# Turning the rotated queries and keys with SBUF transfers and VectorE's block transpose instead of on TensorE

## The chip, the cores and the metric

The kernel runs on one core of one Trainium2 chip. Its time is the device time of the whole program in microseconds (us), median of several runs. The engines are TensorE (PE: matmuls, and PEld: its weight loads), VectorE (DVE), ScalarE (ACT), GpSimd (POOL) and SyncE (SP), whose queue issues nearly all DMAs. SBUF and PSUM have 128 partitions; PSUM is one tensor `bank` of 8 banks of 512 floats.

## The reference

One sequence of 256 tokens with 1024 features goes through two layers of the hybrid block below, then through an attention and pooling block, a state-space and convolution block, and final norms. All is float32. The change lies in the two hybrid layers:

```
h = rmsnorm(x);  z = h @ w_in                     # 1024 x 5888
aq, ak, av, rq, rk, rv, rg, ga, gb = split(z)
aq, ak = rope_half(aq), rope_half(ak)             # 8 query heads, 2 key heads of 64
ya = sliding_window_attention(aq, ak, av) @ w_a   # window 128, 4 query heads for a key head
rq, rk = rotation of pairs(rq), same(rk)          # 4 heads of 128
r  = retention(rq, rk, rv)                        # (rq rk^T * decay) rv, in chunks of 128
yb = (norm(r) * silu(rg)) @ w_b
x  = x + (sigmoid(ga) * ya + sigmoid(gb) * yb) @ w_out
x  = x + relu(rmsnorm(x) @ w_up)^2 @ w_down
```

The scores `aq ak^T` and `rq rk^T` contract over the features of a head, so on PE both operands must stand with their features on the partitions. The product with w_in leaves them with tokens on the partitions. They have to be turned in between.

## The kernel before, in words

**Products.** Every product is computed from operands split in an upper and a lower part: three matmuls for one. The weights come in pieces of 128 x 4 x 512 floats (1 MB): SP loads piece p (line 655), ACT writes its upper part w_hi (line 1466), DVE its remainder w_lo (line 1863), and PE multiplies (lines 745 to 781). Four raw buffers form a ring: the load of piece p waits until DVE has split piece p - 4. Three split buffers form another: ACT's split of p waits until PE has used p - 3. The split halves run ahead of PE by two pieces (`step(p)` splits p + 2).

**Groups.** In a layer w_in has 12 groups of 512 columns (the fourth, AKV, 256), each of two pieces and two token tiles t of 128: RQ, RK, AQ, AKV, RV0, RV1, RG0, RG1, GA0, GA1, GB0, GB1, numbered 0 to 11. PE runs one group after the other, and after each a `window(l, g)`: the small matmuls and transposes of attention and retention. The windows of ACT and DVE run in their own order, one group later (`window(l, g - 1)` in group g). Each engine runs its instructions strictly in the order written; semaphores connect them.

**Rotation.** After groups 0 and 1 `rotate_pairs` turns rq and rk by their angles: tile 0 on DVE, with splits 7 and 8 between its steps, tile 1 on POOL. Its last two steps (lines 575 and 576) write the result back into z_ret, 1024 floats a token: 8 heads of 128. After groups 2 and 3 `rotate_halves` does the same with aq and ak (lines 590 to 600), into z_att and `ak_twice`, in which each key head stands twice.

**Turning.** In window 3 (line 975) PE transposes the 16 blocks of 128 x 128 of z_ret into four banks; in window 4 (line 986) 12 blocks of z_att and ak_twice into three. ACT copies four of the seven banks to SBUF, DVE three (lines 1547 to 1553, 1980 and 1985), as rqT, rkT, aqT and akT. In window 5 PE multiplies the retention scores (line 995), which DVE multiplies by the decay (1989), and the first attention scores (lines 1012 and 1014), on which DVE and ACT run the softmax (1937 to 1956, 1570). In group 6 and 7, RG0 and RG1, DVE evacuates PE's two output banks (line 2117), and PE's next group waits for that. Line 1032 transposes the softmax's result, line 704 belongs to the convolution at the end of the kernel: it moves 16 blocks of 32 partitions from SBUF to SBUF.

**SP.** SP's queue holds the loads in the order of their pieces, and no other DMA in this part of a layer.

Of the kernel before, what the change touches and what calls it, by code (L numbers as in the profile page):

```python
# [31 lines left out]
RET_V = 256  # L32

# [126 lines left out]
def build_program(nc, ins, consts, where, out):  # L160
    ctx = ExitStack()
    with ctx:
# [118 lines left out]
        ak_twice = area(16896, T, KV_HEADS * 2 * HEAD)  # L281
# [111 lines left out]
        ret_turned = sem("ret_turned")  # L393
        rqT_ready = sem("rqT_ready")
        rkT_ready = sem("rkT_ready")
        att_turned = sem("att_turned")
        aqT_first = sem("aqT_first")
        aqT_second = sem("aqT_second")
        akT_ready = sem("akT_ready")
# [156 lines left out]
        def rotate_pairs(eng, o, l, t, tmp, between=lambda part: None):  # L556

            for g in (RQ, RK):
                eng.wait_ge(out_free[t], l * USES + g + 1)
            heads = 2 * RET_HEADS  # L560
            z = z_ret[:, t, :]
            zp = z.rearrange("p (n d e) -> p n d e", n=heads, e=2)
            cos = tab("ret_cos")[:, t * RET_QK:(t + 1) * RET_QK].unsqueeze(1).broadcast_to([P, heads, RET_QK])
            sin = tab("ret_sin")[:, t * RET_QK:(t + 1) * RET_QK].rearrange("p (d e) -> p d e", e=2)[:, :, 0]
            sin = sin.unsqueeze(1).broadcast_to([P, heads, RET_QK // 2])
            a, b = tmp[:, 0, :], tmp[:, 1, :]
            bp = b.rearrange("p (n d e) -> p n d e", n=heads, e=2)
            o.mark(eng.tensor_tensor(a.rearrange("p (n d) -> p n d", n=heads), z.rearrange("p (n d) -> p n d", n=heads), cos, ALU.mult))
            ap = a.rearrange("p (n d e) -> p n d e", n=heads, e=2)
            between(0)  # L570
            o.mark(eng.tensor_tensor(bp[:, :, :, 0], zp[:, :, :, 1], sin, ALU.mult))
            o.mark(eng.tensor_tensor(bp[:, :, :, 1], zp[:, :, :, 0], sin, ALU.mult))
            between(1)
            o.settle()
            o.mark(eng.tensor_tensor(zp[:, :, :, 0], ap[:, :, :, 0], bp[:, :, :, 0], ALU.subtract))
            eng.tensor_tensor(zp[:, :, :, 1], ap[:, :, :, 1], bp[:, :, :, 1], ALU.add).then_inc(rot_done[t], 1)
            eng.wait_ge(rot_done[t], l + 1)

        def rotate_halves(eng, o, l, t, tmp):
# [16 lines left out]
            twice = ak_twice[:, t, :].rearrange("p (v c e d) -> p v c e d", v=KV_HEADS, c=2, e=2)  # L596
            for e, op in ((0, ALU.subtract), (1, ALU.add)):
                o.mark(eng.tensor_tensor(z[:, 0:Q_HEADS, e, :], a4[:, 0:Q_HEADS, e, :], b4[:, 0:Q_HEADS, e, :], op))
                for c in range(2):
                    last = eng.tensor_tensor(twice[:, :, c, e, :], a4[:, Q_HEADS:, e, :], b4[:, Q_HEADS:, e, :], op)  # L600
                    if e == 0 or c == 0:
                        o.mark(last)
# [7 lines left out]
        def _(sp):  # L610
# [46 lines left out]

            for l in range(DEPTH):
                for g in range(W_IN_GROUPS):
                    for half in range(2):  # L660
                        load(w_in_piece(l, g, half))
                for c in range(2):
                    load(square_piece(ins["w_a"][l], c, 0))
# [65 lines left out]
        def _(pe):  # L729
# [233 lines left out]
            def window(l, g):  # L963
# [3 lines left out]
                if g == 3:  # L967
                    if l == 0:
                        pe.wait_ge(vec_ready, 3)
                    for t in (1, 0):  # L970
                        pe.wait_ge(rot_done[t], l + 1)
                        for i in range(4):
                            for j in (2 * i, 2 * i + 1):
                                c = (j % 2) * SEQ + t * P
                                last = pe.transpose(TURN[i][:, c:c + P], z_ret[:, t, j * P:(j + 1) * P], ident)
                            if t == 0:
                                last.then_inc(ret_turned, 1)
                if g == 4:
                    for t in range(T):
                        pe.wait_ge(rope_done[t], l + 1)  # L980
                    pe.wait_ge(rqT_ready, 2 * l + 1)
                    for b, src, n in ((2, z_att, 0), (5, z_att, 2), (3, ak_twice, 0)):
                        for j in range(2):
                            for t in range(T):
                                c = j * SEQ + t * P
                                last = pe.transpose(bank[:, b, c:c + P], src[:, t, (n + j) * P:(n + j + 1) * P], ident)
                        last.then_inc(att_turned, 1)
                if g == 5:
                    pe.wait_ge(rqT_ready, 2 * l + 2)
                    pe.wait_ge(rkT_ready, 2 * l + 2)  # L990
                    pe.wait_ge(akT_ready, l + 1)
# [6 lines left out]
                    pe.wait_ge(aqT_first, l + 1)  # L998
                    pe.wait_ge(aqT_second, l + 1)
# [454 lines left out]
        def _(act):  # L1454
# [86 lines left out]
            def window(l, g):  # L1541
                if l == 0 and g == 1:
                    vectors_turned()
                if g == 3:
                    for i in range(2):
                        act.wait_ge(ret_turned, 4 * l + i + 1)
                        act.activation(rqT[:, 2 * i:2 * i + 2, :].rearrange("p h t -> p (h t)"), TURN[i], copy)\
                           .then_inc(rqT_ready, 1)
                if g == 4:
                    act.wait_ge(att_turned, 3 * l + 1)  # L1550
                    act.activation(aqT[:, 0:2, :].rearrange("p i t -> p (i t)"), bank[:, 2, :], copy).then_inc(aqT_first, 1)
                    act.wait_ge(att_turned, 3 * l + 3)
                    act.activation(akT[:, :, :].rearrange("p i t -> p (i t)"), bank[:, 3, :], copy).then_inc(akT_ready, 1)
# [299 lines left out]
        def _(dve):  # L1853
# [116 lines left out]

            def window(l, g):
# [5 lines left out]
                if g == 3:  # L1977
                    for i in range(2, 4):
                        dve.wait_ge(ret_turned, 4 * l + i + 1)
                        dve.tensor_copy(rkT[:, 2 * (i - 2):2 * (i - 2) + 2, :].rearrange("p h t -> p (h t)"), TURN[i])\  # L1980
                           .then_inc(rkT_ready, 1)
                    rotate_halves(dve, order, l, 0, z_ga)
                if g == 4:
                    dve.wait_ge(att_turned, 3 * l + 2)
                    dve.tensor_copy(aqT[:, 2:4, :].rearrange("p i t -> p (i t)"), bank[:, 5, :]).then_inc(aqT_second, 1)
                if g == 5:
                    for n in range(T):
# [102 lines left out]
            for l in range(DEPTH):  # L2090
# [12 lines left out]
                for g in range(W_IN_GROUPS):  # L2103
                    if g == 4:
                        window(l, g - 1)
                    if g != AKV and (l or g):
                        step(p + 2 * g)
                    if l == 0 and g == 1:
                        spread_dt()
                    if g != 4:  # L2110
# [548 lines left out]
```

## Time and profile before

| | |
|---|---|
| median of 3 runs | 1018.91 us (1018.56 to 1019.53) |
| span of the profiled execution, first to last instruction | 1017.5 us |
| the profiled execution's own time | the page gives its span alone; the runs' median is 1.4 us above it |
| busy: PE, DVE, ACT, POOL | 99%, 70%, 50%, 17% |
| DMA queue of SP | 180.32 MB, 52.8% of the 16 engines' span |

A busy share says how much of the span an engine had instructions in flight. PE's instructions overlap: a matmul that is listed with 0.39 us may follow the one before after 0.23 us, so what a group costs is read from its start to the start of what follows. In a timeline row the bracket at the end gives idle time before the instruction and what ended it.

### The profile page before, as it was taken

To read this page: it belongs to the slowest core of one execution; us is meant where nothing else is said; L and a number is where in the kernel's file an instruction comes from. 1 tells how busy PE (TensorE), PEld (TensorE's weight loads), DVE (VectorE), ACT (ScalarE), POOL (GpSimd) and SP (SyncE) were. 2 spreads that over 40 slices of the span, in tenths; PEclk is the share of its full clock that TensorE was granted. 3 is DMA by queue.
4 is the path that set the end of the run, shared out by engine and by line. 5 is a ranking of instruction groups with operands and counts; after the bars stand their busy time and mean duration, and the time that the engine had idled before them with its cause. 6 is when DMAs were issued, how large, how long until landed. Compare 5 with 4: busy or idle time off the path is not lost.

```text
span 1017.5 us, 13670 instructions
## 1 busy us (share of the span) xinstructions
PE 1010.2 (99%) x5709; PEld 856.6 (84%) x5709; DVE 715.8 (70%) x819; ACT 506.0 (50%) x624; POOL 170.8 (17%) x129
## 2 busy tenths in 40 slices
PE   9999999999999999999999999999999999999997
PEld 8888788888888888888788888888887899899786
DVE  5767755766566565786755767888877767789974
ACT  6545544355444445454564355444467545554352
POOL 0520010000000000430000011000000139259730
PEclk9999999999999999999999999999999999999999
DMA  9763444555556555554444457556553654345451
GB/s 339 246 218 130 166 166 143 178 175 198 183 198 195 178 169 183 186 207 166 158 134 164 166 145 259 203 196 205 190 188 135 223 192 166 124 164 146 116 187 42
DMA packets 98046, 181.29 MB, mean 178 GB/s; under 512 B 8680, under 2 KB 13888, under 8 KB 97856
## 3 DMA queue, kind: packets, MB, share of 16 engines
q1 hardware_dynamic: 97808, 180.32, 52.8%
q8 instruction: 45, 0.74, 0.3%
q14 instruction: 17, 0.14, 0.0%
q10 hardware_dynamic: 176, 0.09, 0.0%
HBM read 177.02 MB, written 1.05 MB: 175 GB/s over the span
## 4 chain that ended last, share of the span: by engine, by line
PE 96%; DMA 2%; DVE 0%; ACT 0%; SPq 0%; issue 0%; DVEq 0%; ACTq 0%
PE bank L745 14%; PE bank L747 12%; PE bank L748 12%; PE bank L1072 11%; PE bank L770 9%; PE bank L774 8%; PE bank L781 8%; PE bank L1076 6%; PE bank L1154 2%; DMA raw<-in_w_in 2%; PE bank L1378 1%; PE bank L943 1%; PE bank L752 1%; PE bank L762 1%; PE bank L1365 1%; PE bank L772 1%
## 5 line engine op out<-in xcount | busy, mean ns | idle before, releaser
L1863 DVE TENSOR_TENSOR w_lo<-arena,w_hi 128x2048 fp32r<-128x2048 f32 (+1 forms) x80 | 185.3, 2325 | 107.5 <-ACT w_hi L1466 107.1
L1863 DVE TENSOR_TENSOR w_lo<-raw,w_hi 128x2048 fp32r<-128x2048 f32 (+1 forms) x78 | 181.2, 2333 | 92.1 <-ACT w_hi L1466 92.0
L1466 ACT ACTIVATE w_hi<-raw 128x2048 fp32r<-128x2048 f32 (+1 forms) x83 | 157.0, 1892 | 105.4 <-PE bank L748 71.5
L1466 ACT ACTIVATE w_hi<-arena 128x2048 fp32r<-128x2048 f32 (+1 forms) x80 | 151.3, 1891 | 105.1 <-PE bank L748 81.3
L1072 PE MATMUL bank<-hT,w_hi 128*128 128x512 f32 x504 | 123.4, 391 | 0.0
L745 PE MATMUL bank<-w_hi,hT 128*128 128x512 f32 (+1 forms) x296 | 114.1, 386 | 0.0
L1072 PEld LDWEIGHTS bank<-hT,w_hi 128*128 128x128 f32 x504 | 92.2, 188 | 17.5
L2465 POOL TENSOR_TENSOR rstd<-mean,const 128x1 f32<-128x1 f32 (+1 forms) x16 | 9.1, 578 | 557.5 <-DVE mean L1872 388.4
L748 PE MATMUL bank<-w_hi,hT 128*128 128x512 f32 (+1 forms) x256 | 97.9, 382 | 0.0
L747 PE MATMUL bank<-w_lo,hT 128*128 128x512 f32 (+1 forms) x256 | 97.9, 382 | 0.0
L770 PE MATMUL bank<-w_hi,hT 128*128 128x512 f32 (+1 forms) x216 | 84.0, 391 | 0.5 <-ACT arena L1478 0.5
L774 PE MATMUL bank<-w_hi,hT 128*128 128x512 f32 (+1 forms) x216 | 82.1, 382 | 0.0
L745 PE MATMUL bank<-w_hi,uT_hi 128*128 128x512 f32 x192 | 74.9, 390 | 0.0
L748 PE MATMUL bank<-w_hi,uT_lo 128*128 128x512 f32 x192 | 74.7, 389 | 0.0
L747 PE MATMUL bank<-w_lo,uT_hi 128*128 128x512 f32 x192 | 74.7, 389 | 0.0
L1076 PEld LDWEIGHTS bank<-hT,w_lo 128*128 128x128 f32 x504 | 67.0, 191 | 3.9
L1076 PE MATMUL bank<-hT,w_lo 128*128 128x256 f32 x504 | 68.3, 282 | 0.0
L745 PEld LDWEIGHTS bank<-w_hi,hT 128*128 128x128 f32 x296 | 55.7, 188 | 10.9
L770 PE MATMUL bank<-w_hi,uT_hi 128*128 128x512 f32 x160 | 62.5, 391 | 0.0
L774 PE MATMUL bank<-w_hi,uT_lo 128*128 128x512 f32 x160 | 62.5, 390 | 0.0
L781 PE MATMUL bank<-w_lo,hT 128*128 128x512 f32 (+1 forms) x216 | 56.1, 382 | 0.0
L748 PEld LDWEIGHTS bank<-w_hi,hT 128*128 128x128 f32 x256 | 48.1, 188 | 9.4
(350 smaller groups left out, 1899.0 us busy)
## 6 DMA issues: line engine op xcount, KB each, us to landing
arena<-in_w_in SPq DMA_DIRECT2D x22, 1024.0 KB, 5.0
raw<-in_w_in SPq DMA_DIRECT2D x20, 1024.0 KB, 5.0
arena<-in_w_up SPq DMA_DIRECT2D x16, 1024.0 KB, 5.3
raw<-in_w_up SPq DMA_DIRECT2D x16, 1024.0 KB, 5.2
arena<-in_w_down SPq DMA_DIRECT2D x16, 1024.0 KB, 5.0
raw<-in_w_down SPq DMA_DIRECT2D x16, 1024.0 KB, 5.0
raw<-in_e_w_in SPq DMA_DIRECT2D x6, 1024.0 KB, 5.1
arena<-in_e_w_in SPq DMA_DIRECT2D x6, 1024.0 KB, 5.1
```

Source lines behind the costliest of these rows:

```text
L745: pe.matmul(dst, a_hi, b_hi, start=first, stop=False, skip_group_check=shared)
L747: pe.matmul(dst, a_hi, b_lo, start=False, stop=False, skip_group_check=shared)
L748: mm = pe.matmul(dst, a_lo, b_hi, start=False, stop=last_one, skip_group_check=shared)
L752: pe.matmul(dst, a_hi, b_lo, start=False, stop=False, skip_group_check=shared)
L770: pe.matmul(dst, a_hi, b_hi, start=(start and i == 0), stop=False, skip_group_check=shared)
L774: pe.matmul(dst, a_lo, b_hi, start=False, stop=False, skip_group_check=shared)
L781: mm = pe.matmul(dst, a_hi, b_lo, start=False, stop=last_one, skip_group_check=shared)
L1072: pe.matmul(UP[j], w_hi[:, s[i], kk, at[j]], hT[:, k, :, :].rearrange("p e t -> p (e t)"), start=(i == kk == 0), stop=False, skip_group_ch ...
L1076: return pe.matmul(UP[j][:, 0:SEQ], w_lo[:, s[i], kk, at[j]], hT_hi[:, i * KP + kk, :], start=False, stop=(i == 1 and kk == KP - 1), skip_ ...
L1154: last = pe.matmul(OUT[t], a[:, KP * i + k, at[t]], w[:, s[i], k, :], start=(first and k == 0), stop=(last_one and k == KP - 1))
L1466: act.activation(w_hi[:, p % SPLIT_RING, :, 0:n], raw_at(p)[:, :, 0:n], copy).then_inc(hi_ready, 1)
L1863: dve.tensor_tensor(w_lo[:, s, :, 0:n], raw_at(p)[:, :, 0:n], w_hi[:, s, :, 0:n].bitcast(F32), ALU.subtract).then_inc(lo_ready, 1)
```

## The change

PE's 28 transposes of a layer and the seven bank copies are gone. For each of the two operands a chain of three steps takes their place. First, the last step of each rotation writes the features in another order: z_ret is then four runs of 256 floats, one for each block b of 32 features, holding that block of all eight heads; the halves go to a new area `a_rows` with four runs of 192 floats (four pairs of query heads and the two key heads, doubled). Second, SP moves run b of the token rows 32i to 32i + 31 to the partitions 32b to 32b + 31 of slot i: sixteen transfers for i and b from 0 to 3, both token tiles in each, 64 KB a transfer for the retention operand, 48 KB for the attention operand. They stand in SP's order after the loads of pieces 12 and 13 (retention, i = 0, 1 and 2, 3) and of 14 and 15 (attention), and wait for both rotations of their operand. Third, one DVE block transpose (32 x 32 blocks) per operand writes `rT` and `aT`, which lie where rqT and rkT, and aqT and akT lay. DVE waits for the sixteen retention transfers at the head of group 5, ahead of split 12, and for the attention transfers behind split 12, ahead of split 13. PE's window 5 waits for rT_ready ahead of the retention scores, and for aT_ready ahead of the attention scores.

```diff
 rotate_pairs, last two steps (rotate_halves likewise, into a_rows)
-            o.mark(eng.tensor_tensor(zp[:, :, :, 0], ap[:, :, :, 0], bp[:, :, :, 0], ALU.subtract))
-            eng.tensor_tensor(zp[:, :, :, 1], ap[:, :, :, 1], bp[:, :, :, 1], ALU.add).then_inc(rot_done[t], 1)
+            to = z.rearrange("p (b n d e) -> p n b d e", b=BLOCKS, n=heads, e=2)
+            a5, b5 = (v.rearrange("p n (b d) e -> p n b d e", b=BLOCKS) for v in (ap, bp))
+            o.mark(eng.tensor_tensor(to[:, :, :, :, 0], a5[:, :, :, :, 0], b5[:, :, :, :, 0], ALU.subtract))
+            eng.tensor_tensor(to[:, :, :, :, 1], a5[:, :, :, :, 1], b5[:, :, :, :, 1], ALU.add).then_inc(rot_done[t], 1)
...
 SP
+            def move_rows(i, dst, src, width, done):
+                rows_i = slice(i * BLOCK, (i + 1) * BLOCK)
+                for b in range(BLOCKS):
+                    rows_b = slice(b * BLOCK, (b + 1) * BLOCK)
+                    sp.dma_start(dst[rows_b], src[rows_i, :, b * width:(b + 1) * width]).then_inc(done, 16)
+            def blocks_moved(l, piece):
+                if piece in (12, 13):
+                    for t in range(T):
+                        sp.wait_ge(rot_done[t], l + 1)
+                    for i in (2 * piece - 24, 2 * piece - 23):
+                        move_rows(i, r_moved.rearrange("p (t i) x -> p t i x", t=T)[:, :, i, :], z_ret, 2 * RET_HEADS * BLOCK, r_blocks)
+                if piece in (14, 15):
+                    for t in range(T):
+                        sp.wait_ge(rope_done[t], l + 1)
+                    for i in (2 * piece - 28, 2 * piece - 27):
+                        move_rows(i, a_moved.rearrange("p (t i) x -> p t i x", t=T)[:, :, i, :], a_rows, A_SLOTS * BLOCK, a_blocks)
...
                         load(w_in_piece(l, g, half))
+                        blocks_moved(l, 2 * g + half)
...
 PE, window
-                if g == 3: 16 transposes of z_ret
-                if g == 4: 12 transposes of z_att and ak_twice
                 if g == 5:
+                    pe.wait_ge(rT_ready, l + 1)
...
+                    pe.wait_ge(aT_ready, l + 1)
...
 DVE
+            def turn_blocks(dst, src, slots):
+                return dve.transpose(dst.rearrange("p s (u q) -> p u s q", q=BLOCK), src.rearrange("p u (s f) -> p u s f", s=slots))
...
+                    if g == 5:
+                        dve.wait_ge(r_blocks, 16 * BLOCKS * BLOCKS * (l + 1))
+                        turn_blocks(rT, r_moved, 2 * RET_HEADS).then_inc(rT_ready, 1)
                     if g != AKV and (l or g):
                         step(p + 2 * g)
...
+                    if g == 5:
+                        dve.wait_ge(a_blocks, 16 * BLOCKS * BLOCKS * (l + 1))
+                        turn_blocks(aT, a_moved, A_SLOTS).then_inc(aT_ready, 1)
```

## Rows read from the trace of the kernel before

**Rows 1.** The page: busy times, granted clock in 40 slices, chain that ended last.

```profile
PE 1010.2 (99%) x5709; PEld 856.6 (84%) x5709; DVE 715.8 (70%) x819; ACT 506.0 (50%) x624; POOL 170.8 (17%) x129
...
PEclk9999999999999999999999999999999999999999
...
PE 96%; DMA 2%; DVE 0%; ACT 0%; SPq 0%; issue 0%; DVEq 0%; ACTq 0%
```

**Rows 2.** Waits of PE in all (engine, line, waited for: us, times, longest).

```profile
PE bank L850 <- DVE h_sb L1897: 1.0, 1, 1.0
```

**Rows 3.** Timeline of PE at its transposes (start, us, engine, line, operation).

```profile
48.32 1.91 PE L975 MATMUL bank<-const,arena 128*128 128x128 f32 x16
...
49.99 0.48 PE L770 MATMUL bank<-w_hi,hT 128*128 128x512 f32 x1
...
61.01 1.47 PE L986 MATMUL bank<-const,arena 128*128 128x128 f32 x12
...
446.78 1.47 PE L986 MATMUL bank<-const,arena 128*128 128x128 f32 x12
...
448.01 0.48 PE L770 MATMUL bank<-w_hi,hT 128*128 128x512 f32 x1
```

**Rows 4.** Timeline of DVE in layer 1.

```profile
433.88 0.69 DVE L576 TENSOR_TENSOR arena<-arena 128x512 f32<-128x512 f32 x1
...
436.81 1.28 DVE L1980 COPY arena<-bank 128x512 f32<-128x512 f32 x2
...
438.01 1.00 DVE L590 TENSOR_TENSOR arena<-arena,const 128x640 f32<-128x640 f32 x1
...
444.07 4.49 DVE L1863 TENSOR_TENSOR w_lo<-raw,w_hi 128x2048 fp32r<-128x2048 f32 x2
...
449.51 2.29 DVE L1863 TENSOR_TENSOR w_lo<-arena,w_hi 128x2048 fp32r<-128x2048 f32 x1 [0.94 <-ACT w_hi L1466]
...
451.72 0.68 DVE L1985 COPY arena<-bank 128x512 f32<-128x512 f32 x1
...
463.95 1.28 DVE L1989 TENSOR_TENSOR arena<-bank,const 128x512 f32<-128x512 f32 x2
...
473.79 1.28 DVE L2117 SCALAR_TENSOR_TENSOR arena<-arena,bank 128x512 f32<-128x512 f32 x2
```

**Rows 5.** Timeline of SP's queue: DMA issues.

```profile
436.92 0.37 SPq L655 DMA_DIRECT2D arena<-in_w_in  x1
...
607.41 0.98 SPq L677 DMA_DIRECT2D arena<-in_o_c_re  x1
...
928.88 5.28 SPq L704 DMA_DIRECT2D arena<-arena  x8
```

**Rows 6.** Line 704, the SBUF to SBUF transfers (issue ns min/median/max; landing).

```profile
L704 SPq DMA_DIRECT2D arena<-arena x16: 591/607/1078, 928.9 to 940.1; - x16
...
DMA to landing us min/median/max: 2.8/5.0/8.8
```

**Rows 7.** Two-microsecond stretches: busy of each engine, clock, DMA share, GB/s.

```profile
942.00:944.00 2.00, 2.00 (x20) 1.87 (x22) 1.91 (x2) 0.57 (x1) 0.76 (x1) 1.00 1.08 195
```

**Rows 8.** The page's DMA issues (count, size, us from issue to landing).

```profile
raw<-in_w_in SPq DMA_DIRECT2D x20, 1024.0 KB, 5.0
```

**Rows 9.** Timeline of ACT in layer 1, splits of pieces 13 and 14.

```profile
453.84 1.92 ACT L1466 ACTIVATE w_hi<-arena 128x2048 fp32r<-128x2048 f32 x1 [3.39 <-PE bank L748]
...
459.81 1.90 ACT L1466 ACTIVATE w_hi<-raw 128x2048 fp32r<-128x2048 f32 x1
```

**Rows 10.** Timeline of POOL, the last step of its rotation.

```profile
443.18 0.78 POOL L600 TENSOR_TENSOR arena<-arena 128x64 f32<-128x64 f32 x2
```

**Rows 11.** Timeline of PE from group 5 to group 7.

```profile
459.02 1.95 PE L995 MATMUL bank<-arena 128*128 128x128 f32 x16
...
460.90 0.49 PE L1012 MATMUL bank<-arena 64*128 64x128 f32 x4
...
475.28 0.48 PE L770 MATMUL bank<-w_hi,hT 128*128 128x512 f32 x1
```

More of the change, by code:

```diff
@@ L32 @@
 RET_V = 256
+BLOCK = 32
+BLOCKS = P // BLOCK
+A_SLOTS = PAIRS + KV_HEADS
 ATT2_HEADS = 4
@@ L280, in build_program @@
         s_ret = area(15872, T, RET_HEADS * P)
-        ak_twice = area(16896, T, KV_HEADS * 2 * HEAD)
+        rT = area(13312, 2 * RET_HEADS, SEQ)
+        aT = area(11776, PAIRS + KV_HEADS, SEQ)
+        r_moved = area(5632, T * BLOCKS, 2 * RET_HEADS * BLOCK)
+        a_moved = area(15360, T * BLOCKS, A_SLOTS * BLOCK)
+        a_rows = area(16896, T, BLOCKS * A_SLOTS * BLOCK)
         probs = area(18432, 2, 384)
@@ L392, in build_program @@
         rope_done = [sem(f"rope_done{t}") for t in range(T)]
[L393 to L399, printed above, removed]
+        r_blocks = sem("r_blocks")
+        rT_ready = sem("rT_ready")
+        a_blocks = sem("a_blocks")
+        aT_ready = sem("aT_ready")
         tanh_ready = sem("tanh_ready")
@@ L595, in rotate_halves @@
             o.settle()
-            twice = ak_twice[:, t, :].rearrange("p (v c e d) -> p v c e d", v=KV_HEADS, c=2, e=2)
+            to = a_rows[:, t, :].rearrange("p (c e s d) -> p s c e d", c=2, e=2, s=A_SLOTS)
+            aq, bq = (v[:, 0:Q_HEADS, :, :].rearrange("p (i c) e d -> p i c e d", c=2) for v in (a4, b4))
             for e, op in ((0, ALU.subtract), (1, ALU.add)):
-                o.mark(eng.tensor_tensor(z[:, 0:Q_HEADS, e, :], a4[:, 0:Q_HEADS, e, :], b4[:, 0:Q_HEADS, e, :], op))
+                o.mark(eng.tensor_tensor(to[:, 0:PAIRS, :, e, :], aq[:, :, :, e, :], bq[:, :, :, e, :], op))
                 for c in range(2):
-                    last = eng.tensor_tensor(twice[:, :, c, e, :], a4[:, Q_HEADS:, e, :], b4[:, Q_HEADS:, e, :], op)
+                    last = eng.tensor_tensor(to[:, PAIRS:, c, e, :], a4[:, Q_HEADS:, e, :], b4[:, Q_HEADS:, e, :], op)
                     if e == 0 or c == 0:
@@ L966, in window @@
                     turn_vectors()
-                if g == 3:
+                if g == 5:
+                    pe.wait_ge(rT_ready, l + 1)
                     if l == 0:
                         pe.wait_ge(vec_ready, 3)
[L970 to L991, printed above, removed]
                     for n in range(T):
@@ L997, in window @@
                         last.then_inc(s_ret_done, 1)
-                    pe.wait_ge(aqT_first, l + 1)
-                    pe.wait_ge(aqT_second, l + 1)
+                    pe.wait_ge(aT_ready, l + 1)
                 if g == 6:
@@ L1543, in window @@
                     vectors_turned()
[L1544 to L1553, printed above, removed]
                 if 6 <= g < 6 + PAIRS:
@@ L1977, in window @@
                 if g == 3:
[L1978 to L1981, printed above, removed]
                     rotate_halves(dve, order, l, 0, z_ga)
-                if g == 4:
-                    dve.wait_ge(att_turned, 3 * l + 2)
-                    dve.tensor_copy(aqT[:, 2:4, :].rearrange("p i t -> p (i t)"), bank[:, 5, :]).then_inc(aqT_second, 1)
                 if g == 5:
+                    dve.wait_ge(aT_ready, l + 1)
                     for n in range(T):
@@ L2109, in _ @@
                         spread_dt()
+                    if g == 5:
+                        dve.wait_ge(a_blocks, 16 * BLOCKS * BLOCKS * (l + 1))
+                        turn_blocks(aT, a_moved, A_SLOTS).then_inc(aT_ready, 1)
                     if g != 4:
```

## The prediction, made before the changed kernel ran

> **What bounds the kernel now.** I read the page first: the busy shares, the chain that ended last and the granted clock [rows 1]. TensorE (PE) is busy for 99% of the span, the chain that ended last is 96% PE, and the clock is at its upper level (2.4 GHz) in all 40 slices. The waits of PE come next: the longest is 1.0 us at the very start [rows 2]. So in both layers PE is the engine that sets the end, each microsecond of PE work taken out is a microsecond gained, and each wait that PE is given is a microsecond lost. The timelines of PE, VectorE (DVE), ScalarE (ACT), GpSimd (POOL) and SyncE's queue (SP) around the change give the rest. I work in the times of layer 1, whose rows are shown; layer 0 has the same pattern 385.8 us earlier (446.78 - 61.01) [rows 3]. Pieces are numbered inside the layer: group g of w_in uses pieces 2g and 2g+1.
>
> **What goes.** On PE, 16 transposes after group 3 (1.67 us from the first to the next matmul, 49.99 - 48.32) and 12 after group 4 (1.23 us, 448.01 - 446.78) [rows 3]; 2.90 us a layer, 5.8 us in all, every bit of it on the path. On DVE go the two copies after group 3 (1.20 us from their start to that of the next instruction) and one of 0.68 us after group 4 [rows 4]. ACT loses four copies; ACT waits for PE around there, so they are worth nothing. The cosine and sine products stay and the last two steps of each rotation write the same number of elements to other places; I count nothing, since the rotations are followed by slack on the paths below unless they grew by over 0.5 us.
>
> **What comes.** SP issues 32 SBUF to SBUF transfers a layer: sixteen for the retention operand (64 packets of 1 KB each, 64 KB), sixteen for the attention operand (64 packets of 768 B, 48 KB), in batches of eight behind the loads of pieces 12, 13, 14 and 15. DVE gets two block transposes, of 2048 and of 1536 elements per partition. PE gets two waits, DVE two, SP two kinds. What is queued behind them: on SP the loads of pieces 13 to 16, on DVE the weight splits 12 and 13, then the scores' softmax and the evacuations of group 6, on PE everything.
>
> *Price of an issue.* The nearest row is the sixteen SBUF to SBUF transfers late in this kernel, also 32 partitions each with three dimensions on both sides: 0.607 us of SP each, and 0.66 from one to the next (eight in 5.28 us) [rows 5, 6]. The loads cost 0.37 [rows 5] (0.41 with the gap), the dearest comparable small transfer 0.98 [rows 5]. I take 0.66, since it shares source, destination and partition count; 0.41 and 0.98 are the ends.
>
> *Price of the data.* The first of those transfers (142 KB) landed 2.8 us after issue [rows 6], and with the DMA engines full they moved 195 GB/s [rows 7]. That is 0.33 us for 64 KB and 0.25 for 48 KB: less than the 0.66 that SP takes to issue one, so SP's issuing sets the pace. A load lands 5.0 us after issue [rows 8].
>
> A rule that speaks against this change is in the Trainium skill (SBUF — State Buffer, "Door 1: The DMA port swizzle"): a transfer whose partitions are 0 to 31 reaches only 8 of 16 ports, with an asymptote of about 218 GB/s; the trace agrees, with 195. By the page's figure the sixteen 64 KB transfers would be 4.8 us (an estimate) and by the row 5.4; both lie below the issue time.
>
> *Price of a block transpose.* No row shows one. DVE's split of 2048 elements takes 2.21 us from start to start, two of them 4.49 [rows 4]. At that rate the two turns cost 2.2 and 1.7 us. The lower end is half of that (1.1 and 0.85), the upper end twice the split's, 4.4 and 3.4, for an instruction that reorders and of which no row is seen. I take 2.2 and 1.7. The Trainium skill (Vector Engine (DVE) Microarchitecture Reference, "The reshape front-end and per-opcode configuration") says that the transposing array sustains one element per cycle and lane; that agrees with the rate I took, and no run here shows it yet.
>
> **The sum, step by step in layer 1.**
> 1. Rotation of token tile 0 ends at 433.88 + 0.69 = 434.6 on DVE [rows 4]. SP issues retention batch one from 434.6 to 439.9 (8 x 0.66), load 13 to 440.3 (before it was issued at 436.9 [rows 5]; its split by ACT starts at 453.8 [rows 9], 2.9 us earlier now, and it lands by 446, so this costs nothing), batch two to 445.6.
> 2. DVE: without the two copies the rotation of halves and split 10 run 1.2 us earlier, split 10 ends at 445.1, split 11 at 447.3. PE starts group 5 at 446.78 - 1.67 = 445.1 and needs split 10 some 1.9 us later: no stall. POOL's half of the rotation ends at 443.18 + 0.78 = 444.0 [rows 10], before SP gets to it.
> 3. The last retention transfer is issued at 444.9 and lands at about 447.5. DVE arrives at 447.3, turns until 449.7, splits piece 12 until 451.9: as before (449.51 + 2.29 = 451.8 [rows 4]). This wait is free.
> 4. SP: load 14 until 446.0, attention batch one until 451.3, load 15 until 451.7, batch two until 457.0. Its eighth is issued at 456.3. It lands 2.8 us later, less 0.4 for the smaller size: 458.7. (By the data: load 15 lands at 456.3, eight transfers of 0.25 behind it end at 458.3. The same.)
> 5. DVE has stood at that wait since 451.9. It turns until 460.5.
> 6. PE: group 5 takes 11.0 us (448.01 to 459.02), so it ends at 456.1; the retention products, 1.88 us [rows 11], are done at 458.0. Then PE waits for the turned attention operand until 460.6: **a stall of 2.6 us**, and the scores start 0.3 us before their old 460.90 [rows 11]. Nearly the whole gain is given back here.
> 7. DVE comes late to what follows. Splits 13 and 14 run from 460.5 to 464.9. Piece 14 is not ACT's fault: its upper part was done at 461.7 and now is earlier [rows 9]. The decay multiply starts at 464.95 instead of 463.95 [rows 4], 1.0 us late, and the softmax and evacuation chain up to the first evacuation of group 6 runs without slack worth naming (473.79 + 0.6 = 474.4 before [rows 4]). It ends at 475.4, PE wants the bank at 475.28 - 0.3 = 475.0 [rows 11]: **a second stall of about 0.5 us**. Group 7 starts at 475.5, 0.2 us later than before. From there each chain had 2 us or so of slack or follows PE.
>
> Per layer +0.2 us, twice +0.4 us. The profiled execution's span was 1017.5 us, 1.4 below the median of the runs (1018.91); that part lies around the span and does not change. 1018.9 + 0.4 = **1019.3 us**.
>
> **The rivals.**
> *A, the issues are cheap* (0.41 each, like a load). Then SP is idle before load 14, which waits for split 10 at 445.1; attention batch two is issued by 452.6, and the data set the pace: load 14 off the engines at about 449, 2.0 us of transfers, load 15 2.6, 2.0 more and 1.0 to report: 456.6. Turned at 458.4; PE stalls 0.4, DVE is 1.05 us early at the decay multiply, PE then waits 0.6 at group 7. Net -1.85 a layer, 1015.2 us. For it: 64 packets per transfer instead of 128. Against it: a load has 512 packets and costs 0.37, so the count of packets is not what costs. No stall at all would be -5.8, 1013.1 us: the bound.
>
> *B, slower: the wait for the attention blocks grows.* The place is step 6, the price is one for one beyond 2.9 us of stall, and it decides from an issue interval of 0.66 on: 31 issues stand one behind the other between 434.6 and the last, so each further 0.1 us costs PE about 3 us a layer. At 0.8 the last attention transfer is issued at 460.6 and lands at 463.0, the scores start 3.9 us late, group 7 adds 0.4: +8.6 us in all, 1027.5. At 0.98 it is issued at 466.2, and the time is 1038.7. For it: within the second batch of the late transfers issues stretched up to 1.08 us [rows 6] while a load was ahead of them in the queue, as one is here. Against it: the first batch kept to 0.66, and these transfers are a third to a half of the size.
>
> *C, slower: a block transpose at half rate.* Turn two ends at 462.1 and the decay multiply starts 2.6 us late; scores +1.3, group 7 +0.5: +3.6 us in all, 1022.5. Nothing in the trace speaks for or against it.
>
> That PE's transposes would still be there is no rival: the code that issues them is gone. A clock that falls in a stall of several microseconds would make B worse; the trace of before has no stall that could show it [rows 1, 2].
>
> **How the numbers follow.** From no change a measurement of this kernel can tell about 0.2%, 2.0 us. My forecast 0.42, all of it within 2 us; A 0.25, faster; B 0.20 and C 0.13, slower. Range for 8 in 10: 1014.6 (below A's value, above its bound) to 1026.0 (C, and B up to an interval of about 0.77).
>
> **What would show it.** Right: L975 and L986 gone, PE waiting two to three microseconds before its first score matmul of each layer, with the DVE transpose as releaser, DVE idle for some 6 us ahead of the 1536-element transpose with a DMA as releaser, SP issuing without a break from the end of the rotation for 22 us, a short PE wait for the DVE evacuation at group 7. Wrong: no PE wait at the scores (then A), a wait of over 4 us or one before the retention products (then B), a transpose of over 3 us (then C). The forecast is also wrong if a load of pieces 13 to 17 arrives too late for ACT, which I count at nothing because the nearest, 13 and 14, have about 5 us to spare.

## The result: 1026.95 us, slower than before

The changed kernel takes 1026.95 us (four runs, 1024.84 to 1028.65) against 1018.82 (four runs of the kernel before beside them): ratio 1.0079, 95% interval [1.0064, 1.0093]. The forecast was 1019.3, the range ended at 1026.0. The profiled execution took 1025.95 us, of which the span is 1024.0, 6.5 us more than the span of before; the four runs' median is 1.0 us above it.

The page of the changed kernel, for [rows 1]: PE's share falls from 99 to 98%, one slice of the clock shows less than full, and DVE, DMA and SP are now on the chain that ended last.

```profile
PE 1008.5 (98%) x5653; PEld 853.1 (83%) x5653; DVE 721.9 (70%) x817; ACT 502.2 (49%) x616; POOL 170.7 (17%) x129
...
PEclk9999999999999999998999999999999999999999
...
PE 90%; DVE 4%; DMA 3%; SPq 2%; issue 1%; ACT 1%; DVEq 0%; ACTq 0%
```

PE's waits, for [rows 2]: the first line is new, one wait a layer, 4.4 and 3.8 us, for the turned attention operand.

```profile
PE bank L1018 <- DVE arena L1969: 8.3, 2, 4.4
PE bank L878 <- DVE h_sb L1893: 1.0, 1, 1.0
```

The chain of work in layer 0, from split 10 on (start, length, what; some of the issues left out). I tell layer 0 from here; 385.8 us lie between its times and those of layer 1 in the kernel before. After split 10 comes the load of piece 14, then issue after issue on SP's queue, the flight of the last block, the turn, and the scores.

```profile
58.02 2.30 DVE w_lo L1859
60.34 0.37 SPq L662
...
60.81 0.59 SPq L670
...
65.94 0.59 SPq L662
...
66.62 0.59 SPq L670
...
71.11 3.21 DMA arena<-arena
74.35 1.79 DVE arena L1969
```

DVE's timeline, for [rows 4]: the two block transposes take 2.31 and 1.78 us; before the second DVE stands still for 7.4 us. The first product of the rotation of halves takes 2.20 us instead of 1.00 [rows 4].

```profile
50.75 2.20 DVE L596 TENSOR_TENSOR arena<-arena,const 128x640 f32<-128x640 f32 x1
...
62.43 2.31 DVE L1969 STREAM_TRANSPOSE arena<-arena 128x2048 f32<-128x2048 f32 x1
...
74.35 1.78 DVE L1969 STREAM_TRANSPOSE arena<-arena 128x1536 f32<-128x1536 f32 x1 [7.43 <-DMA arena<-arena]
```

PE's timeline, for [rows 11]: retention products, wait, scores, group 6. In the windows under it the granted clock is the third number from the right: it falls to its lower level (1.2 GHz) while PE stands still and stays there for 6.8 us (the share of each window that is missing from 1.00, counted double). While it is low, the eight products from 77.76 to the L809 group take 3.52 us; the same eight of group 6's second token tile take 1.81 at the upper level.

```profile
69.82 1.95 PE L1002 MATMUL bank<-arena 128*128 128x128 f32 x16
76.18 0.80 PE L1018 MATMUL bank<-arena 64*128 64x128 f32 x4 [4.41 <-DVE arena L1969]
...
77.76 0.79 PE L798 MATMUL bank<-w_hi,hT 128*128 128x512 f32 x1
...
81.28 1.08 PE L809 MATMUL bank<-w_lo,hT 128*128 128x512 f32 x4
```

```profile
72.00:76.00 4.00, 0.00 (x0) 0.00 (x0) 1.65 (x1) 0.51 (x1) 0.00 (x0) 0.80 0.52 151
76.00:80.00 4.00, 3.82 (x13) 2.75 (x14) 4.00 (x3) 0.00 (x0) 0.00 (x0) 0.50 0.49 148
80.00:84.00 4.00, 4.00 (x16) 3.24 (x15) 3.83 (x8) 0.00 (x0) 0.00 (x0) 0.85 1.00 375
```

Layer 0 then adds up, beside these rows of the kernel before:

```profile
73.25 1.95 PE L995 MATMUL bank<-arena 128*128 128x128 f32 x16
75.13 0.49 PE L1012 MATMUL bank<-arena 64*128 64x128 f32 x4
...
75.98 0.50 PE L770 MATMUL bank<-w_hi,hT 128*128 128x512 f32 x1
...
77.96 1.08 PE L781 MATMUL bank<-w_lo,hT 128*128 128x512 f32 x4
```

The retention products start 3.43 us earlier than before (69.82 against 73.25; 0.29 of it lies ahead of the change, 3.14 are the missing transposes). From their start to the scores it takes 6.36 us instead of 1.88, 4.48 more, of which the wait is 4.41. The scores take 1.58 us instead of 0.85, and the first eight products of group 6 take 3.52 instead of 1.98. That is -3.43 + 4.48 + 0.73 + 1.54 = +3.32 us; group 7 starts at 92.86 against 89.51, +3.35. Layer 1 adds 3.17, with a wait of 3.84.

### The profile page after: what moved, and what is told of

It is laid out like the page before. It is cut to its first block, busy times and chain, and to the rows that moved or that the text cites. A ratio compares the mean times of both kernels' runs of the same rounds, so it can differ in the third digit from the quotient of the medians.

```text
span 1024.0 us, 13617 instructions
## 1 busy us (share of the span) xinstructions
PE 1008.5 (98%) x5653; PEld 853.1 (83%) x5653; DVE 721.9 (70%) x817; ACT 502.2 (49%) x616; POOL 170.7 (17%) x129
## 3 DMA queue, kind: packets, MB, share of 16 engines
HBM read 177.02 MB, written 1.05 MB: 174 GB/s over the span
## 4 chain that ended last, share of the span: by engine, by line
PE 90%; DVE 4%; DMA 3%; SPq 2%; issue 1%; ACT 1%; DVEq 0%; ACTq 0%
PE bank L773 13%; PE bank L775 11%; PE bank L776 11%; PE bank L1078 11%; PE bank L798 8%; PE bank L802 7%; PE bank L809 7%; PE bank L1082 6%; PE bank L1160 2%; DMA raw<-in_w_in 2%; PE bank L1384 1%; DVE w_lo L1859 1%; SPq L670 1%; PE bank L971 1%; PE bank L780 1%
## 5 line engine op out<-in xcount | busy, mean ns | idle before, releaser
L773 PEld LDWEIGHTS bank<-w_hi,hT 128*128 128x128 f32 x296 | 55.6, 188 | 11.0
L809 PE MATMUL bank<-w_lo,hT 128*128 128x512 f32 (+1 forms) x216 | 56.2, 382 | 0.0
L775 PEld LDWEIGHTS bank<-w_lo,hT 128*128 128x128 f32 x256 | 48.1, 188 | 9.4
## 6 DMA issues: line engine op xcount, KB each, us to landing
arena<-in_w_in SPq DMA_DIRECT2D x22, 1024.0 KB, 5.2
raw<-in_w_in SPq DMA_DIRECT2D x20, 1024.0 KB, 5.3
arena<-in_w_up SPq DMA_DIRECT2D x16, 1024.0 KB, 5.7
raw<-in_w_up SPq DMA_DIRECT2D x16, 1024.0 KB, 5.2
arena<-in_w_down SPq DMA_DIRECT2D x16, 1024.0 KB, 5.1
raw<-in_w_down SPq DMA_DIRECT2D x16, 1024.0 KB, 5.1
raw<-in_e_w_in SPq DMA_DIRECT2D x6, 1024.0 KB, 5.2
arena<-in_e_w_in SPq DMA_DIRECT2D x6, 1024.0 KB, 5.2
```

Of the source, the lines that this page charges most:

```text
L773: pe.matmul(dst, a_hi, b_hi, start=first, stop=False, skip_group_check=shared)
L775: pe.matmul(dst, a_hi, b_lo, start=False, stop=False, skip_group_check=shared)
L809: mm = pe.matmul(dst, a_hi, b_lo, start=False, stop=last_one, skip_group_check=shared)
```

## The experiments

The theory going in: *SP's issuing makes the attention blocks late, PE stands still for them, and in standing still loses its clock as well.* Its rivals: the data of the transfers, DVE's chain behind the wait, a cost of the transfers to the loads. A time is the median of a kernel's runs; a ratio is taken to the runs of the kernel before that were made beside them (medians 1018.67, 1019.08 and 1018.84 us).

### Filling PE's wait

```diff
+                    keep_clock(2, 24)          # 24 products of the identity
                     pe.wait_ge(aT_ready, l + 1)
```

> PE is given 24 matmuls of the identity (128x128, some 0.11 us each, 2.6 us) between the retention scores and its wait for the turned attention operand; nothing else changes and nothing reads their result. Theory 1, the clock: in the changed kernel PE stands still for 4.4 and 3.9 us there, the granted clock then falls to its lower level for 6.8 us, and the first matmuls of group 6 take 1.6 us longer and the scores 0.7 (2.3 us a layer). With the filler the remaining idle time is below 2 us, the clock stays at its upper level, the first score matmul starts as late as before (the wait is for a DMA), and the time is 1026.9 - 2 x 2.3 = 1022.3 us. Theory 2, PE is slow after the wait because its data or SBUF's ports are busy with the transfers and loads: the granted clock may change but the slow stretch stays, 1027.

Measured: 1024.04 us (1023.26 to 1024.38), ratio 1.0051 [1.0036, 1.0066]. The clock never fell, but the filler took 5.5 us, longer than the wait, and so delayed PE itself: the scores start 0.4 us after the end of the turn in layer 0 and 1.5 us after it in layer 1. So a shorter one was tried.

> As the filler before, with 18 instead of 24 products of the identity. The first filler took 5.5 us and so outlasted the wait by 0.8 us in each layer; 18 take 4.1 us and end before it. Theory 1, the clock: without that own delay the time is 1024.0 - 2 x 0.8 = 1022.4 us, granted clock at its upper level throughout. Theory 2, something else slows PE after the wait: 1024 or more.

Measured: 1022.59 us (1021.90 to 1023.31), ratio 1.0035 [1.0022, 1.0048]. Its PE timeline and a window of it: filler, 0.57 us of wait, scores as late as in the changed kernel and at full speed, clock 1.00. (In layer 1 it still outlasts the wait, by 0.4 us.)

```profile
71.46 4.18 PE L878 MATMUL bank<-const 128*128 128x128 f32 x36
76.21 0.49 PE L1019 MATMUL bank<-arena 64*128 64x128 f32 x4 [0.57 <-DVE arena L1970]
```

```profile
76.00:80.00 4.00, 3.79 (x21) 2.97 (x22) 4.00 (x3) 0.00 (x0) 0.00 (x0) 1.00 0.38 103
```

So of the 8.1 us that the change costs, about 4 (1026.95 - 1022.59 = 4.4) are the clock's, and they come back with useless work in the wait. The two kernels did not run side by side; a second set of runs of the changed kernel (1026.10, below) makes it 3.5, and its profile 4.6 (0.73 + 1.54 in layer 0, as much in layer 1). The Trainium skill (TensorE: Matmul & The Clock Gate, Part 1) says that the gate lowers the clock after PE has been idle and raises it after it has been busy; the trace agrees: the clock is down from within the wait of 4.41 us until 81.2, 5 us after PE has started again.

With the clock up, PE meets another wait, 0.44 us at the start of group 7 in layer 0, which the changed kernel does not have. It is put down to ACT's split, which here runs behind the softmax and ends within 0.1 us of DVE's first evacuation:

```profile
91.23 0.47 PE L798 MATMUL bank<-w_hi,hT 128*128 128x512 f32 x1 [0.44 <-ACT w_hi L1473]
```

### One operand at a time

Retention by transfers and block transpose, attention on PE as before:

```diff
-            to = a_rows[:, t, :] ...                     # rotate_halves writes z_att, ak_twice again
-                if piece in (14, 15): ...                # no attention transfers
+                if g == 4: 12 transposes of z_att and ak_twice, three copies
-                    pe.wait_ge(aT_ready, l + 1)
```

> Only the retention operand goes by the sixteen transfers and the block transpose; the attention operand is transposed on PE as in the kernel before. Theory 1, only the attention operand's chain is late: the retention operand is turned some 7 us before PE wants it, its transfers and the 2.2 us turn are hidden, and the 16 transposes are a clean gain of 1.7 to 1.9 us a layer: 1018.8 - 3.5 = 1015.3 us, PE without a wait in the layers. Theory 2, the transfers themselves cost (they delay weight loads, or DVE's 2.2 us more a layer delays its splits): the gain is eaten, 1018 or more.

Measured: 1015.29 us (1015.12 to 1015.54), ratio 0.9966 [0.9954, 0.9979]; PE has no wait in the layers. Its DVE timeline has the 2.31 us turn and split 12 behind it (first two rows); they end at 66.8, and DVE's next split in the kernel before (the third row) comes after 3.39 us in which it stood still:

```profile
62.33 2.31 DVE L1982 STREAM_TRANSPOSE arena<-arena 128x2048 f32<-128x2048 f32 x1
64.56 2.25 DVE L1872 TENSOR_TENSOR w_lo<-raw,w_hi 128x2048 fp32r<-128x2048 f32 x1
```

```profile
70.02 2.29 DVE L1863 TENSOR_TENSOR w_lo<-raw,w_hi 128x2048 fp32r<-128x2048 f32 x1 [3.39 <-ACT w_hi L1466]
```

A clean 3.4 us, 1.7 a layer: the price of 16 transposes, with 2.2 us more of DVE and 1 MB more of SBUF traffic hidden.

Attention by transfers, retention on PE as before (the mirror of that edit):

> Only the attention operand goes by transfers and block transpose; the retention operand is transposed on PE as before. Theory 1, SP's issuing behind the load that waits for split 10 sets the landing, whatever the retention transfers did: that load is issued at about 446.4 in layer 1's times of before, 16 issues of 0.64 and a load follow, the last lands near 460, the turned operand is there at 461.5; PE arrives at 459.7, waits 1.5 to 2 us with its clock up, and is about 0.5 to 1.0 us late per layer: 1020 to 1021 us. Theory 2, the 1 MB of retention data ahead in the queue is what made the attention blocks late: without it they land 2 us or more earlier, there is no wait, and the 12 transposes are gained, 1016.3.

Measured: 1025.01 us (1022.57 to 1025.60), ratio 1.0057 [1.0042, 1.0072]. SP's queue, DVE's turn and PE's wait in layer 0:

```profile
60.38 0.37 SPq L661 DMA_DIRECT2D arena<-in_w_in  x1
60.86 5.23 SPq L669 DMA_DIRECT2D arena<-arena  x8
...
66.82 6.08 SPq L669 DMA_DIRECT2D arena<-arena  x8
```

```profile
74.83 1.78 DVE L1978 STREAM_TRANSPOSE arena<-arena 128x1536 f32<-128x1536 f32 x1 [9.04 <-DMA arena<-arena]
```

```profile
76.67 0.49 PE L1022 MATMUL bank<-arena 64*128 64x128 f32 x4 [3.07 <-DVE arena L1978]
```

With no retention transfer in the kernel the blocks land at 74.8, no earlier than with sixteen of them (74.35). The retention transfers ahead of load 14 do not matter; the chain starts at that load, at the end of split 10. The time came out 4 us above what I expected. In the profiled execution (1022.57) PE waits 3.1 and 1.6 us with its clock up, 1.6 us above my number; the other three took 1024.8 to 1025.6 at a mean granted clock of 0.995 or 0.996. So a wait of 3 us seems to cost the clock in some executions (the slower three have no profile).

The two parts do not add up: alone they are worth -3.4 and +6.3 us, together +8.1. The attention blocks land at the same time either way, so the PE time that the retention part frees only makes the wait for them longer (4.41 us instead of 3.07, the scores at 76.18 instead of 76.67), and the longer wait costs the clock in both layers.

### Issues or data

The changed kernel with `part=2` for the attention operand, each transfer moving the first half of its row run (a memset of the area at the start of the kernel stands in for the rest):

> The changed kernel with half of the bytes in each attention transfer (24 KB, packets of 384 B); the other half of the block is left out of the computation (it is zero in layer 0 and stale in layer 1). Issues, waits and order stay. Theory 1, issuing sets the pace: the last block lands within 0.5 us of where it did (74.4 in layer 0), the time is 1026 to 1027. Theory 2, data set the pace: 196 KB less in each batch at 195 GB/s is 1 us each, the last lands 1 to 2 us earlier, PE waits 3 us, and the time is 1020 to 1024.

Measured: 1025.43 us (1024.28 to 1027.72), ratio 1.0066. SP's second batch and the turn:

```profile
66.69 5.76 SPq L671 DMA_DIRECT2D arena<-arena  x8
```

```profile
74.13 1.78 DVE L1970 STREAM_TRANSPOSE arena<-arena 128x1536 f32<-128x1536 f32 x1 [7.14 <-DMA arena<-arena]
```

Half of the bytes gone, and the last block lands 0.22 us earlier. At this place issuing sets the pace. The time, 1025.43, lies between the ranges of the two theories; I decide by the landing, since the runs (1024.28 to 1027.72) differ with their clock (0.996 to 0.993).

### The place in SP's queue, and a second queue

Each attention batch one load earlier (`if piece in (13, 14)`), with split 13 ahead of DVE's wait:

> The whole change, with split 13 ahead of DVE's wait, and each attention batch one load earlier in SP's queue (behind load 13 and load 14 instead of 14 and 15). Theory 1: batch one starts when batch two of the retention operand is out, at 59.6 in layer 0 instead of 60.8, and load 15 is no longer ahead; the last is issued at about 69.9 and lands at 73; PE waits about 3 us instead of 4.4, its scores start 0.3 us before those of the kernel before. 1018 us where the clock stays up through the wait, up to 1023 where it falls. Theory 2, the place in the queue does not matter: 1026 to 1027.

Measured: 1022.71 us (1019.19 to 1024.64), ratio 1.0033 [1.0016, 1.0049]. PE waits 3.3 and 3.1 us in the profiled execution, and its time again hangs on the clock. In layer 1 it falls within the wait, for 6.8 us. In layer 0 it falls only after it: the first scores run at full speed, and the clock is down from 76.1 for 3.4 us.

```profile
75.36 0.49 PE L1018 MATMUL bank<-arena 64*128 64x128 f32 x4 [3.34 <-DVE arena L1969]
...
76.24 0.79 PE L798 MATMUL bank<-w_hi,hT 128*128 128x512 f32 x1
```

The six runs, time and mean granted clock of the core:

```
1019.19 0.999   1020.60 0.998   1021.81 0.996
1023.62 0.993   1023.98 0.995   1024.64 0.993
```

The second eight transfers on ACT's queue, with split 13 ahead of DVE's wait:

```diff
+                if g == 4:                               # ACT's window, behind its split 12 in the code's order
+                    for t in range(T):
+                        act.wait_ge(rope_done[t], l + 1)
+                    for i in (2, 3):
+                        for b in range(BLOCKS):
+                            act.dma_start(moved[...], a_rows[...]).then_inc(a_blocks, 16)
```

> The whole change, with split 13 ahead of DVE's wait, and the second eight attention transfers issued by ACT's queue (after its split 12, where it stands idle) instead of SP's. Theory 1, one queue's issuing at 0.64 us each is what makes the blocks late: SP issues its eight until 65.9 in layer 0, ACT its eight from 61.7 to 66.8; the last lands by about 70, the operand is turned at 71.8 to 72.5, PE comes at 71.8 and waits less than 1 us, the clock stays up, and what the 28 transposes free is gained: 1012 to 1014 us. Theory 2, the data set the pace (the 16 engines are shared): the last block lands about when it did, 74.4, and the time is 1023 to 1027.

Measured: 1013.52 us (1012.96 to 1014.15), ratio 0.9946 [0.9930, 0.9963]: the fastest version of this study, 13.4 us below the changed kernel. ACT's queue issues beside its own split (59.85 to 61.8), SP's at the same time; DVE turns at 69.89, and PE goes from the retention products to the scores without a wait (0.7 us are left in layer 1). Two things changed at once here: eight issues run on another queue, and no load stands between the two batches. The version before says that an earlier place in SP's queue alone does not do it (1022.71).

```profile
59.85 1.91 ACT L1472 ACTIVATE w_hi<-raw 128x2048 fp32r<-128x2048 f32 x1
60.52 4.63 ACTq L1557 DMA_DIRECT2D arena<-arena  x7
```

```profile
69.89 1.78 DVE L1978 STREAM_TRANSPOSE arena<-arena 128x1536 f32<-128x1536 f32 x1 [0.39 <-DMA arena<-arena]
```

```profile
69.94 1.95 PE L1002 MATMUL bank<-arena 128*128 128x128 f32 x16
71.82 0.49 PE L1018 MATMUL bank<-arena 64*128 64x128 f32 x4
```

Eight and four on SP (one load earlier and behind load 14), four on ACT:

> As the version with ACT's queue, but spread otherwise: ACT issues only the last four attention transfers, SP eight directly behind the retention transfers (one load earlier) and four behind load 14. Theory 1 (issuing sets the pace, each queue in parallel): SP's last goes out at about 67.3 in layer 0 and, behind load 14, lands at 70.5, so the operand is turned at 72.3; PE waits about 0.5 us: 1013 to 1014.5 us, no better than eight and eight. Theory 2: if the engines' data set the pace in this regime, moving the blocks ahead of load 14 lands them earlier than with eight and eight (69.9), and the last 0.7 us of wait in layer 1 goes: 1012.5.

Measured: 1018.96 us (1017.18 to 1023.71), ratio 1.0003 [0.9991, 1.0015], some 5 us above what I expected. SP's last four are out at 67.8, the last of them issued at 67.2, as computed, but the landing of these four took 4.3 to 5.2 us, and DVE turns at 72.44, so PE waits 2.8 us.

```profile
64.61 0.59 SPq L662 DMA_DIRECT2D arena<-in_w_in  x1
65.30 2.51 SPq L670 DMA_DIRECT2D arena<-arena  x4
```

```profile
72.44 1.78 DVE L1977 STREAM_TRANSPOSE arena<-arena 128x1536 f32<-128x1536 f32 x1 [3.62 <-DMA arena<-arena]
```

They were issued right behind a 1 MB load. The changed kernel has the same at the head of a batch: there the first transfer behind a load lands 5.1 us after its issue and the eighth 3.2 us (2.2 in layer 1). Four issues are over before the landings have come down, so here the issues do not set the pace; that it is the load's data they wait for fits the times and is not tested. In the version of eight and eight SP's eight are out at 66.1, before the next load.

### DVE's chain behind the wait

In the changed kernel, the wait and turn of the attention operand moved behind `step(p + 2 * g + 1)`:

> The changed kernel with one thing moved: DVE splits piece 13 before it waits for the attention blocks instead of after it. Theory 1, the landing and the clock are the whole cost: the split goes into the 7 us in which DVE stands idle, the turn is as late as before, PE's stall and the slow clock stay, and since PE is slowed there DVE's following chain is not the limit: 1026.5 to 1027. Theory 2 (step 7 of the prediction), the chain from split 13 over 14 to the softmax and the evacuation of group 6 delays PE as well: 1 to 2 us less a layer, 1023 to 1025.

Measured: 1026.91 us (1024.69 to 1027.20), ratio 1.0076 [1.0061, 1.0091]. Split 13 does go into DVE's idle time, and nothing is gained where the clock falls.

```profile
65.21 4.53 DVE L1859 TENSOR_TENSOR w_lo<-raw,w_hi 128x2048 fp32r<-128x2048 f32 x2
75.03 1.78 DVE L1969 STREAM_TRANSPOSE arena<-arena 128x1536 f32<-128x1536 f32 x1 [5.29 <-DMA arena<-arena]
```

The same question where nothing stalls, eight and eight with the old order:

> The eight and eight version with DVE's order as in the changed kernel: split 13 behind the turn of the attention operand. Where PE stands still 4 us and its clock falls, moving the split brought nothing (1026.91 against 1026.95). Theory 1: here, with no stall ahead, DVE's chain (turn, splits 13 and 14, decay multiply, softmax, evacuation of group 6) is what is late next, as step 7 of the prediction has it: it starts 1 to 1.5 us later and PE waits for the evacuation 0.5 to 1 us a layer, 1014.5 to 1015.5 us. Theory 2: that chain never limits PE, 1013.5 us.

Measured: 1013.73 us (1013.66 to 1014.28), against 1013.52: no difference that the runs can tell. In its profile DVE is 0.75 us later at the decay multiply (75.62 against 74.87) and 2.05 us in layer 1, and PE has a wait at the start of group 7 that the version with the other order does not have, 0.34 us and 0.28 in layer 1, as with the filler:

```profile
86.40 0.47 PE L798 MATMUL bank<-w_hi,hT 128*128 128x512 f32 x1 [0.34 <-ACT w_hi L1472]
```

The changed kernel once more:

> The changed kernel itself once more, on the chip on which the others of this call run. Both theories: about 1027 us where the clock falls in both layers, with single runs 2 us lower where it falls in one; it gives the distance to the versions beside it on one chip.

Measured: 1026.10 us (1024.98 to 1027.17), ratio 1.0073 [1.0056, 1.0090]; 12.4 us above the last version (1013.73), which ran beside it. In the profiled execution (1025.32) the clock falls in both layers, but in layer 1 for half as long and after the wait, not in it. The scores run at full speed there, the clock is down from 466.2 for 3.4 us, and the first eight products of group 6 take 3.52 us: 1.5 us lost instead of 2.3.

```profile
465.23 0.49 PE L1018 MATMUL bank<-arena 64*128 64x128 f32 x4 [4.39 <-DVE arena L1969]
...
466.09 0.76 PE L798 MATMUL bank<-w_hi,hT 128*128 128x512 f32 x1
```

```profile
464.00:466.00 2.00, 0.77 (x8) 0.52 (x8) 2.00 (x2) 0.00 (x0) 0.00 (x0) 1.00 1.03 397
466.00:468.00 2.00, 2.00 (x7) 1.53 (x6) 2.00 (x2) 0.00 (x0) 0.00 (x0) 0.54 0.04 12
```

## Why the prediction was wrong

It had the mechanism: the transposes' gain given back in a wait for the attention blocks, paced by SP's issues. It failed at step 6, in the size of that wait and, more, in what a wait does to PE: the fall of the clock was put at nothing and cost about 4 of the 7.7 us between forecast and measurement.

- *What goes.* Right in the main. Retention alone gained 3.4 us in two layers (1.7 each, as forecast); both together 5.6 us where they were nearly hidden (1019.08 - 1013.52, with 0.7 us of wait left), of 5.8 forecast. In the profile 3.14 us of PE went in layer 0, not 2.90.
- *Price of an issue.* 0.597 us and 0.64 from one to the next, forecast 0.66. Right, and issue, not data, was the pace (half of the bytes: 0.22 us).
- *Price of a block transpose.* 2.23 and 1.70 us from start to start, forecast 2.2 and 1.7. Rival C is out.
- *Steps 1 to 3.* Right but for step 2: the first product of the rotation of halves took 1.2 us more, so the copies' gain of 1.2 us was lost, split 10 ended at 60.3 (forecast 445.1 - 385.8 = 59.3), and load 14, behind which the blocks stand, went out at 60.34. Without the copies the product starts at 50.75, while POOL runs its own (48.88 to 52.26); with the copies back in place (attention alone) it starts at 52.00, when POOL's is nearly over, and took 1.00 us again. The two fit together; no run tests it.
- *Step 4.* Forecast landing 458.7 - 385.8 = 72.9, measured 74.3. The last issue begins at 71.11 instead of 456.3 - 385.8 = 70.5, 0.6 late since load 14 went out late, and its block flies for 3.2 us instead of 2.4. That this issue takes 1.55 us instead of 0.6 is not a third term: it begins on time, and with 18 filler products, where the last issue is not held up (eight in 5.10 us), the block lands at 74.35 just the same. In layer 1 the flight is 2.2 us and the wait 3.8.
- *Step 6, the size of the wait.* 4.4 us (3.8 in layer 1) instead of 2.6: the landing is 1.4 us later, and PE comes 0.4 us earlier than forecast. The scores start 1.05 us later than before, instead of 0.3 earlier.
- *Step 6 again, what it left out.* I gave the wait its length as price. In fact PE comes out of it at half clock and loses 2.3 us more a layer, out of the 3.3 that a layer got longer. The filler shows it, 4.4 us in two layers. The text named the falling clock under rival B, as a thing that the trace could not show, and gave it no price. The range ended 1 us short for that.
- *Step 7, a second stall of 0.5 us at group 7.* It did not come in the changed kernel, where the slow clock makes PE itself late there. With the clock up it does come, at about the forecast size: 0.44 us with 18 filler products, 0.74 and 0.32 with attention alone, 0.34 and 0.28 with eight and eight in the old order, and none once split 13 stands ahead of the turn. So the step was right in kind. It is too small to show in the times (1013.73 against 1013.52), and the profile puts it down to ACT's split behind the softmax, not to DVE's evacuation.
- *Rival B* came true in its sign, a wait over 4 us (4.41 in layer 0, 3.84 in layer 1), and near its number (1027.5) by luck: its cause, dearer issues, is out (0.64 us from one to the next, it wanted over 0.66), and about half of the loss was the clock. *Rival A* is out, issues behind a load are not cheap.

What stays open: why the last block flies for 3.2 to 3.8 us in layer 0 and 2.2 to 2.6 in layer 1, why a last issue is sometimes held up, and why the clock falls at some waits near 3 us and not at others (in the profiled executions waits up to 2.8 us kept it, of two of 3.1 one kept and one lost it, those of 3.3 and more lost it), sometimes within the wait for 6.8 us and sometimes after it for 3.4.

## What to carry to other kernels

Work moved off the bounding engine is worth its full time as long as its replacement is back early. Look where the replacement's chain starts (here a load that waits for a split, behind which sixteen issues queue on one sequencer), count issues, not bytes, and see whether a large load is queued directly ahead of them. In these runs a wait of PE of 3.1 us or more could cost 1.5 to 2.3 us beyond its length, since the clock fell in it or just behind it; price it with the clock, or fill it. And a cost that hides behind a slower one (the second stall here) comes out when that one is gone. Of a change in two parts try each alone: here one was a clean gain and the other a loss nearly twice as large, together they cost more than their sum, and a second issuing queue made the whole a gain.

## What the runs showed of the hardware

A 32-partition SBUF to SBUF transfer costs its queue 0.6 us of issuing with 128 packets of 1136 B, 64 of 1024, 768 or 384 B alike, against a 1 MB load's 0.37. ACT's queue issues them at 0.62 us each while ACT computes. In the changed kernel an attention transfer (48 KB) directly behind a 1 MB load lands 5.0 to 5.1 us after its issue, the eighth behind it 2.2 to 3.2. The granted clock was down for 6.8 or for 3.4 us at a time; it fell within a wait of PE or up to 0.9 us after its end. A load right behind such a batch costs 0.59 us of issue instead of 0.37. DVE's block transpose of float32 runs at 1.09 ns per element and partition (2.23 us for 2048), the rate of its subtractions. A DVE product of a broadcast operand took 2.20 us when it started in the middle of POOL's own (48.88 to 52.26), and 1.00 when it started in the last 0.3 us of it.
